# Where the statistics of a convolution's layer norm are taken: the last chunk's taps on TensorE, the small sums ahead of the mean, and the first norm's sum of squares inside the second product

## The reference

```
h = rmsnorm(x, g_mix[0])                     # x * rsqrt(mean(x*x)) * g
a = h @ w_pw1 + b_pw1                        # 1024 -> 2048
u = a[..., :D] * sigmoid(a[..., D:])
v = depthwise_conv(concat(history, u), w_dw) + b_dw     # 31 taps, each feature by itself
v = layernorm(v, g_ln, b_ln)                 # mean and variance over 1024 features
y = silu(v) @ w_pw2 + b_pw2 ;  x = x + y
```

## Time and profile before

| | |
|---|---|
| median of 3 runs | 1431.27 us (1430.9 to 1431.3) |
| the profiled execution's own time | 1436.4 us |
| span of the profile | 1434.6 us |
| PE busy | 1387.0 us, 97% of the span |
| DVE busy | 819.7 us, 57% |
| ACT busy | 608.6 us, 42% |
| POOL busy | 729.6 us, 51% |
| mean granted clock of TensorE | 0.983 |

### The profile page before, as it was taken

One profiled execution on the slowest core, in us unless ns is written; L12 is line 12 of the kernel. 1 busy time (PEld: TensorE's weight loads), 2 busy tenths in 40 slices (PEclk: granted clock), 3 DMA queues, 4 the chain that ended last, 5 costly groups with the idle time before them and its releaser, 6 DMA issues.

```text
span 1434.6 us, 29089 instructions
## 1 busy us (share of the span) xinstructions
PE 1387.0 (97%) x12494; PEld 1291.5 (90%) x12494; DVE 819.7 (57%) x1235; ACT 608.6 (42%) x1032; POOL 729.6 (51%) x505
## 2 busy tenths in 40 slices
PE   5999979999999999998899999999999999999997
PEld 5787759999999999998899977677999999999997
DVE  5758666855545455467466665655475545545434
ACT  5212234643444434344456644443364443444432
POOL 2422303368878777443223353340346788888831
PEclk9999969999999999999999999999999999999998
DMA  8312201222332223531111277762122223322221
GB/s 201 84 31 61 63 30 59 89 89 92 105 99 89 89 89 100 184 100 61 56 34 34 96 298 260 274 248 91 60 89 89 89 89 101 106 89 89 89 89 63
DMA packets 123183, 148.70 MB, mean 104 GB/s; under 512 B 13552, under 2 KB 114160, under 8 KB 118832
## 3 DMA queue, kind: packets, MB, share of 16 engines
q1 hardware_dynamic: 115888, 104.90, 23.4%
q0 software_dynamic: 7168, 41.95, 7.8%
HBM read 142.81 MB, written 4.03 MB: 102 GB/s over the span
## 4 chain that ended last, share of the span: by engine, by line
PE 89%; DVE 5%; ACT 2%; POOL 1%; issue 1%; DMA 0%; DVEq 0%; SPq 0%; ACTq 0%; POOLq 0%
PE ps L1564 29%; PE ps L1713 20%; PE ps L1701 18%; PE ps L1844 5%; PE ps L1606 3%; PE ps L1884 3%; PE ps L1933 2%; POOL wl L524 1%; ACT wh L660 1%; PE ps L1779 1%; PE ps L1626 1%; PE ps L1671 1%; PE ps L1614 1%; PE ps L1942 1%; PE ps L1914 1%
## 5 line engine op out<-in xcount | busy, mean ns | idle before, releaser
L524 POOL TENSOR_TENSOR wl<-raw,wh 128x512 fp32r<-128x512 f32 (+2 forms) x252 | 439.9, 1748 | 438.4 <-ACT wh L660 438.3
L660 ACT ACTIVATE wh<-raw 128x512 fp32r<-128x512 f32 (+2 forms) x253 | 192.5, 762 | 373.6 <-PE ps L1564 197.8
L524 POOL TENSOR_TENSOR wl<-wuv,wh 128x512 fp32r<-128x512 f32 x104 | 134.7, 1306 | 89.3 <-ACT wh L660 89.3
L1564 PE MATMUL ps<-xh,wh 128*128 128x272 f32 x704 | 148.8, 292 | 14.6 <-DVE xl L1005 12.4
L1713 PE MATMUL ps<-mh,wh 128*128 128x272 f32 x768 | 158.6, 288 | 0.0
L1713 PE MATMUL ps<-mh,wl 128*128 128x272 f32 x768 | 158.6, 288 | 0.0
L1713 PE MATMUL ps<-ml,wh 128*128 128x272 f32 x768 | 158.3, 288 | 0.0
L1564 PE MATMUL ps<-xh,wl 128*128 128x272 f32 x704 | 145.3, 289 | 0.0
L1564 PE MATMUL ps<-xl,wh 128*128 128x272 f32 x704 | 145.2, 288 | 0.0
L1564 PEld LDWEIGHTS ps<-xh,wh 128*128 128x128 f32 x704 | 110.3, 189 | 25.3 <-POOL wl L524 13.1
L1713 PEld LDWEIGHTS ps<-ml,wh 128*128 128x128 f32 x768 | 120.4, 188 | 0.0
(11 more groups left out here) (306 smaller groups left out, 3076.3 us busy)
## 6 DMA issues: line engine op xcount, KB each, us to landing
raw<-w_up SPq DMA_DIRECT2D x32, 1024.0 KB, 5.4
raw<-w_down SPq DMA_DIRECT2D x32, 1024.0 KB, 5.1
raw<-w_pw SPq DMA_DIRECT2D x16, 512.0 KB, 5.3
raw<-w_pw SPq DMA_DIRECT2D x4, 1024.0 KB, 5.3
raw<-w_o SPq DMA_DIRECT2D x4, 1024.0 KB, 5.1
raw<-w_dq SPq DMA_DIRECT2D x3, 1024.0 KB, 5.3
raw<-w_uq SPq DMA_DIRECT2D x4, 768.0 KB, 4.4
x<-xT SPq DMA_DIRECT2D x4, 544.0 KB, 7.4
```

The costliest lines, as they stand in the source:

```text
L524: pf.tensor_tensor(weight(wl, u), weight_raw(u), f32(weight(wh, u)), ALU.subtract).then_inc(w_lo, 1)
L660: af.activation(weight(wh, u), weight_raw(u), ACT.Copy).then_inc(w_hi, 1)
L1564: m = tf.matmul(ps[:, bank_of(u) + bank, 0:width], w[:, k, :], a[:, k, part], start=(k == 0 and n == 0), stop=(k == nk - 1 and n == 2))
```

## The change

There are three parts.

1. `sums` of the first norm moves from chunk k = 2 of product 2 to chunk k = 6 of product 1.
2. Chunk 7 gets all its 31 taps on TensorE: an eighth group of 12 matmuls, with diagonals built by POOL as 31 instead of 28. `dve_taps(7)` and `shifted(7)` over all tokens go. The sample tokens of chunk 7 alone are shifted by an operation of their own (128 x 32), and the last addition becomes one operation that takes the folded sum, adds the bias and subtracts `mean`.
3. TensorE's list behind chunk 7's taps: the small sums of `acc` and `acc2` come first, then the fold, `mean_part(acc)`, the small sums of chunk 7, and `mean_part` of chunk 7 last. DVE centres no chunk before the reciprocal `rs`; it centres 0 to 2 behind it, 3 and 4 behind `normed_v(0)`, and 5, 6, 7 one by one behind the first three `low`.

```
-        diag = sb("diag", [P, 2, PE_TAPS, SB], F32, conv_mem)
+        diag = sb("diag", [P, 2, TAPS, SB], F32, conv_mem)
+        def pe_taps(c):
+            return PE_TAPS if c < DC - 1 else TAPS
...
-                w = vec[:, VEC["w_dw"] + c * TAPS:VEC["w_dw"] + c * TAPS + PE_TAPS]
+                n = pe_taps(c)
+                w = vec[:, VEC["w_dw"] + c * TAPS:VEC["w_dw"] + c * TAPS + n]
...
-            def shifted(c):
-                link(df.tensor_tensor(v[:, c, :], v[:, c, :], mean[:, :], ALU.subtract))
...
-                dve_taps(c)
                 if c < DC - 1:
+                    dve_taps(c)
                     partial(c)
...
-            shifted(DC - 1)
             add_to(acc[:, :], v[:, k, :], False)
-            partial(DC - 1)
             square_to(acc2[:, :], False)
             dve.sem_inc(stat_in, 1)
+            link(df.tensor_tensor(v[:, DC - 1, NP:T], v[:, DC - 1, NP:T], mean[:, NP:T], ALU.subtract))
+            partial(DC - 1)
             dve.wait_ge(fold_mm, DC)
-            df.tensor_tensor(v[:, DC - 1, 0:NP], v[:, DC - 1, 0:NP], ps[:, conv_bank(DC - 1), :], ALU.add).then_inc(sq_src, 1)
+            df.scalar_tensor_tensor(v[:, DC - 1, 0:NP], ps[:, conv_bank(DC - 1), :], V("b_dw", DC - 1), mean[:, 0:NP],
+                                    ALU.add, ALU.subtract).then_inc(sq_src, 1)
...
-            dve.wait_ge(mean_mm, 1)
-            for c in range(2):
-                centred(c)
...
-            centred(2)
             root_()
             df.reciprocal(rs[:, :], rs[:, :]).then_inc(rs_out, 1)
-            for c in range(3, DC - 1):
+            dve.wait_ge(mean_mm, 1)
+            for c in range(3):
                 centred(c)
...
             normed_v(0)
-            centred(DC - 1)
+            for c in range(3, 5):
+                centred(c)
             for c in range(DC):
                 if c + 1 < DC:
                     low_done()
+                    dve.wait_ge(sq_src, DC + c + 2)
                     normed_v(c + 1)
                 low(ml[:, c, :], (t0, t1)[c % 2][:, :], mh[:, c, :])
+                if c + 5 < DC:
+                    centred(c + 5)
...
-                for s in range(0, PE_TAPS, GROUPS):
+                n = pe_taps(c)
+                for s in range(0, n, GROUPS):
...
-                        for j in range(GROUPS):
+                        for j in range(min(GROUPS, n - s)):
...
-            product(1, xh, xl)
+            product(1, xh, xl, norm_at=6)
             for c in range(DC):
                 if c + 1 < DC:
-                    product(2 * c + 2, xh, xl, norm_at=2 if c == 0 else None)
+                    product(2 * c + 2, xh, xl)
...
-            fold_products(DC - 1)
...
             pe.wait_ge(stat_in, 1)
-            mean_part(acc, True, False)
             small_part(5, 0, acc)
             small_part(5, 1, acc2).then_inc(small_mm, 1)
+            fold_products(DC - 1)
+            mean_part(acc, True, False)
             pe.wait_ge(sq_src, DC)
-            mean_part(v[:, DC - 1, :], False, True).then_inc(mean_mm, 1)
             small_part(4, 0, v[:, DC - 1, :])
             pe.wait_ge(sq_out, 2 * DC)
             small_part(4, 1, sq[:, (2 * DC - 1) % 2, :]).then_inc(small_mm, 1)
+            mean_part(v[:, DC - 1, :], False, True).then_inc(mean_mm, 1)
```

More of the change, by code:

```diff
@@ L561, in diagonals @@
                     pool.wait_ge(conv_mm, c - 1)
-                w = vec[:, VEC["w_dw"] + c * TAPS:VEC["w_dw"] + c * TAPS + PE_TAPS]
-                pf.tensor_tensor(diag[:, c % 2, :, :], ident4.unsqueeze(1).to_broadcast([P, PE_TAPS, SB]),
-                                 w.unsqueeze(2).to_broadcast([P, PE_TAPS, SB]), ALU.mult).then_inc(diag_out, 1)
+                n = pe_taps(c)
+                w = vec[:, VEC["w_dw"] + c * TAPS:VEC["w_dw"] + c * TAPS + n]
+                pf.tensor_tensor(diag[:, c % 2, 0:n, :], ident4.unsqueeze(1).to_broadcast([P, n, SB]),
+                                 w.unsqueeze(2).to_broadcast([P, n, SB]), ALU.mult).then_inc(diag_out, 1)
             low(0)
@@ L1185, in _ @@
             dve.wait_ge(rs_mm, 1)
-            dve.wait_ge(sq_src, 2 * DC - 1)
+            dve.wait_ge(sq_src, DC + 3)
             normed_v(0)
-            centred(DC - 1)
-            dve.wait_ge(sq_src, 2 * DC)
+            for c in range(3, 5):
+                centred(c)
             for c in range(DC):
@@ L1603, in tap_products @@
                     for i in range(GROUPS):
-                        for j in range(GROUPS):
+                        for j in range(min(GROUPS, n - s)):
                             part = slice(SB * i, SB * (i + 1))
                             m = tf.matmul(ps[SB * j:SB * (j + 1), conv_bank(c) + i, :], diag[part, c % 2, s + j, :], ext[part, c, s + j:s + j + NP],
-                                          start=(s == 0), stop=(s == PE_TAPS - GROUPS))
+                                          start=(s == 0), stop=(s + j + GROUPS >= n))
                 m.then_inc(conv_mm, 1)
```

## The result

| | before | changed |
|---|---|---|
| median | 1431.27 us (1430.4 to 1435.99, 5 runs) | 1423.3 us (1422.42 to 1425.13, 5 runs) |
| ratio | | 0.9941, 95% interval 0.9929 to 0.9954 |
| profiled execution, span | 1436.4, 1434.6 us | 1424.49, 1422.7 us |
| mean granted clock in it | 0.983 | 0.987 |

The forecast was 1425.7, range 1423.6 to 1428.4. In the profile the span is 11.9 us shorter, more than the 8.0 of the medians: 0.9 of it lies ahead of TensorE's first matmul, 1.9 from there to the first tap of chunk 0, 7.8 from the taps of chunks 6 and 7 to the third product of `pw2`, and 1.3 behind that product, where nothing was changed. The profiled execution of the kernel before was no typical one: it is 5 us above the median, and it alone cannot say what the change is worth.

What follows compares the result with a forecast made beforehand. TensorE's chain was taken to bound the kernel, with DVE at the layer norm. First stage -2.15, layer norm to third `pw2` product -3.9, clock +0.5: -5.6 us, from 1431.27 to 1425.7; range 1423.6 to 1428.4.

Steps and rivals of the forecast that it cites:

- The first norm: First stage: with `sums` inside product 1, product 3 starts without a wait, at 33.35 instead of 35.51; 2.15 us won.
- first stage gives nothing: Rival: moving `sums` only shifts the wait from product 3 to chunk 0's taps; gain 3.5, time 1427.8; chance 0.09.
- Chunk 7's taps: Layer norm: TensorE's added group of 12 matmuls costs 1.05 us, taps end at 185.47; DVE loses 2.16 us of taps.
- The span model: Chunk 7's taps: the group of 12 would cost nearly the full 1.13 us, making the sum 0.1 worse.
- TensorE's list behind the taps: Layer norm: no wait, clock falling about 3 us behind the taps; sums end at 195.4 instead of 202.0, 6.6 us won.
- From the variance to the pair: Behind the small sums: `mean_part` of chunk 7 precedes the spreading of `rs`; `normed_v(0)` at 199.8 against 206.06, 6.25 us won.
- The pair: `product_pair`: last `low` ends 16.1 us after `normed_v(0)`, giving back 2.4 of 6.25; the clock costs 0.5 more.
- the good case: `product_pair`: the clock returns 4.7 us after the pair's start, by 208, in time and free.
- the bad one: `product_pair`: the clock's return is counted from the fourth `low` at 209.7, which costs 1.65 us.
- early-clock case: Rival: clock falls 4 us behind the taps, back before the fourth `low`; gain 7.1, time 1424.2; chance 0.14.
- The slower case: Rival: clock stays at 1.2 GHz through `product_pair` and one product more; +5.4, time 1436.7; chance 0.04.
- The rule of the Trainium skill on small idle times: Slower rival: small idle times between groups of matmuls can throw the clock back repeatedly; the prediction gave it little weight.

Runs made afterwards that it cites:

- norm_only: Kernel before with only the first norm's `sums` moved to chunk 6 of product 1; ratio 0.9989 to the kernel before.
- early_second: Changed kernel with `normed_v(1)` directly behind `normed_v(0)` and one subtraction between each `low` and the next normed chunk; ratio 0.9938 to the kernel before.
- pool_mean: Changed kernel with the mean copied once by ScalarE and subtracted from chunks 5 to 7 by GpSimd; ratio 0.9932 to the kernel before.
- fill_pair: Changed kernel with three matmuls to no use between the spreading of `rs` and `product_pair`; ratio 0.9951 to the kernel before.
- no_norm: Changed kernel with only the move of the first norm's `sums` undone; ratio 0.9974 to the kernel before.
- small_x4: Changed kernel with the ten small sums of `acc` and `acc2` made four times, three to no use; ratio 1.0046 to the kernel before.
- order_only: Kernel before with the new lists of TensorE and of the centring, chunk 7's last three taps still on VectorE; ratio 1.0000 to the kernel before.
- fold_first: Changed kernel with the fold and half mean ahead of the small sums of `acc` and `acc2`; ratio 0.9956 to the kernel before.
- fold_first_2: The same kernel as fold_first, run again beside the changed kernel; ratio 0.9951 to the kernel before.
- fold_pool: pool_mean with the fold and half mean ahead of the small sums; ratio 0.9943 to the kernel before.
- null: The kernel before run once more, unchanged, as a measure of noise; ratio 0.9996 to the kernel before.

## Why the prediction was wrong, step by step

- **The first norm: right.** No wait ahead of product 3. From TensorE's first matmul to the first tap of chunk 0 it took 29.4 to 29.8 us in the five profiles without part 1, and 26.6 to 27.7 in the twelve with it: 2.3 us won between the means, 2.15 forecast. norm_only's times show 1.6 us with an interval that reaches none. The rival "first stage gives nothing" is refuted by the traces.
- **Chunk 7's taps: right.** From the start of chunk 6's taps to the end of chunk 7's it took 16.2 to 16.3 us with the last three taps on VectorE and 17.2 to 17.6 with the group of 12 on TensorE: 0.9 to 1.35 us, 1.05 forecast. A full group is 1.13, so three column blocks cost about as much as four. The span model of the Trainium skill (TensorE: Matmul & The Clock Gate, Part 3), which the prediction cites, said so. VectorE's 2.9 us went out of the path, and with the new list what had been 3.38 of waiting became none.
- **TensorE's list behind the taps: the step that failed.** "The clock fell 2.2 and 4.1 us after dense work; I take the middle, about 3." With the new list and no gap the fall came 7.5 to 8.3 us behind the taps in five of seven profiles (the changed kernel three times, early_second, pool_mean), 15.4 in fill_pair and 2.9 in no_norm. The sum over the layer norm was built on that middle, and the term mis-sized by it is the time from the taps' end to the last small sum: the sums took 6.6 us behind the taps with a lag of 8 and 9.8 with 2.9; the forecast had 202.00 - 184.42 - 6.6 = 11.0, less the 1.05 of the taps' group, 9.9. The 3.3 us between are the clock's. A second, hidden step is the base: the forecast subtracted from a profile with a lag of 2.2 and carried the result over to a median 5.1 us lower, without asking whether the typical execution has that lag.
- **Why the medians moved by 8.0 and not by 9.7.** Counted from TensorE's first matmul, the third product of `pw2` starts 9.65 us sooner in the changed profile, but that compares a short lag with a long one. At like lags the stretch is 3.3 us shorter (norm_only 51.9, changed 48.6) or 3.8 (before 56.4, no_norm 52.6), and the forecast had 3.4. With 2.3 for the first stage that makes 5.6 to 6.1, against 5.6 forecast. What the medians have beyond the forecast (2.4 us by the first result, 1.8 by the weighted ratio) would then be a shift of the odds towards the long lag: with part 2 in the kernel 11 of 12 profiles have it (small_x4 left out), without part 2 it is 1 of 4. This is argued, not shown: four profiles are few, and no run fixes the lag. The mean granted clocks cannot settle it. They are 0.984 to 0.985 for the kernel before on the later chips and 0.986 to 0.988 for the changed kernel; but the forecast itself shortened the time at 1.2 GHz from 27.3 us to about 20, which alone lifts the mean by 0.0025 (an estimate: half of 7.3 us over the span).
- **From the variance to the pair: right in its path, too long by 0.8.** `mean_part` of chunk 7 stands ahead of the spreading, but at 2.4 GHz it took about 1.1 us instead of 2.02 and ended before `rs` was there; `normed_v(0)` came 3.6 us behind the sums, 4.4 forecast. Three subtractions end before it does, as forecast.
- **The pair: the total near, by two errors that cancel.** From `normed_v(0)` to the third product it took 20.85 us instead of 18.52, 2.3 longer; the forecast had 2.35 and 0.5 for the clock. Its parts were otherwise: the last low part ended 15.1 us behind `normed_v(0)`, not 16.1, so VectorE's subtractions cost 1.4 and not 2.4; and TensorE ended unit 0 2.05 us behind that low part, against 1.17 before, so the clock cost 0.9 and not 0.5. The clock rose 8.2 us behind the pair's start, about midway between the 4.7 of the good case and the 11 or so of the bad one, which counted from the fourth low part.
- **Rivals.** The early-clock case (gain 7.1, "it falls 4 us behind the taps") came nearest and had 0.14; its lag was still too short by half, and its early return of the clock did not come. The slower case did not come near. The rule of the Trainium skill on small idle times (TensorE: Matmul & The Clock Gate, Part 1, second HAM failure mode) is borne out once at most: in no profile did the pair stay at 1.2 GHz, and none lost the clock again once it had risen within the pair; fill_pair, which entered it at 2.4 GHz, lost it 2.2 us in, behind waits of 2.5 and 0.8 us. What six show (order_only, no_norm, small_x4, fold_first, fold_first_2, fold_pool) is another thing: the clock rose over the half mean or the spreading of `rs` and fell again from 1.0 us before to 0.2 us behind the pair's start, over a single wait of 3.4 us or more. In no_norm, small_x4 and fold_first_2 the pair then took 18.0 to 18.1 us.
- **The range.** Its low end was built on a lag of at most 4.1, the longer of two rows. Two rows were no basis for an end.

## What to carry to other kernels

A stretch that TensorE enters warm and leaves cold has a price that one profile cannot give: here the same instructions took 4.4 us more or less by when the clock fell. Take the fall's lag from several executions, or give it a range from none to all of the stretch. Remove the waits of TensorE first; what order its small matmuls have mattered little. And where a wait on one engine is traded for work on another (VectorE's subtractions between the low parts), look for an engine that is idle just there: GpSimd took three of them, and no operation of VectorE became longer; whether that also saves time the medians do not tell.

## What the runs showed of the hardware

- The clock can stay at 2.4 GHz over a wait of 3.3 us of TensorE (norm_only), and it can fall 2.1 to 2.2 us into one of the same length (before, null). Of 17 profiles the lag was 2.1 to 4.3 us in five, 7.2 to 8.6 in eleven and 15.4 in one (fill_pair), and nothing lay between. In the eleven, TensorE did a fold and a half mean at 2.4 GHz between 1.5 and 5.5 us behind the taps; in four of the five short ones nothing of the kind stood ahead of the fall, and in no_norm 0.6 us of the fold did. But norm_only, before and null have the same list, so this does not say what decides; it is left open.
- One-column matmuls did not hold the clock: 4.3 us into a row of them it fell, with PE busy all the time (small_x4). Five such matmuls take 1.16 us at 2.4 GHz and 2.03 at 1.2.
- GpSimd's subtraction of 128x544 took 1.31 us each and slowed none of the VectorE operations beside it, which all had one operand in PSUM (pool_mean). VectorE's L1060, with both tensors in SBUF, took 2.33 us beside GpSimd's L528 and 0.75 where L528 did not run (changed kernel, 40.89 and 32.35).
